# Head pairs on alternating halves of the array, split step sums and later gates in a two-block transformer kernel

## The reference, cut to what matters

```python
proj = u @ w_in
z, xbc, dt_raw, v = split(proj)              # gates, convolution input, steps, pooled input
xbc = silu(causal_depthwise_conv(xbc, conv_w, conv_b))
xs, bm, cm = split(xbc)                      # 16 heads of 64; B and C: 2 groups of 128
dt = softplus(dt_raw + dt_bias); a = -exp(a_log)
a_cs = cumsum(dt * a) in each chunk of 128   # 4 chunks
seg = exp(where(causal, a_cs[l] - a_cs[s], -inf))
y_diag = (C B^T * seg) @ (xs * dt)
y_off  = (C * exp(a_cs)) @ state carried from the chunks before
y = (y_diag + y_off + d_skip * xs) * silu(z)
y_ssd = rmsnorm(y, ssd_norm)
y_pool = multi_scale_pool(v, pool_w, pool_scale)
return concatenate([y_ssd, y_pool]) @ w_out
```

## Time and profile before

| what | value |
|---|---|
| median of 3 runs | 2312.72 us (2311.17 to 2314.09) |
| profiled execution, its own time | 2313.4 us |
| its span | 2311.5 us |
| mean granted PE clock | 0.988 of full speed |
| busy: PE, DVE, ACT, POOL | 97%, 54%, 37%, 14% |

### The profile page before, as it was taken

One profiled execution on the slowest core, in us unless ns is written; L12 is line 12 of the kernel. 1 busy time (PEld: TensorE's weight loads), 2 busy tenths in 40 slices (PEclk: granted clock), 3 DMA queues, 4 the chain that ended last, 5 costly groups with the idle time before them and its releaser, 6 DMA issues. The chain is left out here.

```text
span 2311.5 us, 28724 instructions
## 1 busy us (share of the span) xinstructions
PE 2239.9 (97%) x11284; PEld 1778.9 (77%) x11284; DVE 1248.6 (54%) x1966; ACT 844.3 (37%) x1410; POOL 322.5 (14%) x320
## 2 busy tenths in 40 slices
PE   8899999989999999999999999999999999999998
PEld 6778778858888887877678888887775568888887
DVE  5766566354544445266635454554547874555454
ACT  4433554234222224355532222233135654222223
POOL 1300351001000003032210000010035541000001
PEclk9999999999999999999999999999989999999999
DMA  5232114403333332311123333333230003333231
GB/s 161 73 109 82 47 56 134 121 27 92 94 98 94 98 96 77 91 55 43 31 73 100 101 92 100 93 99 97 91 92 2 2 10 92 99 93 101 91 100 46
DMA packets 292661, 188.08 MB, mean 81 GB/s; under 512 B 7856, under 2 KB 286640, under 8 KB 292528
## 3 DMA queue, kind: packets, MB, share of 16 engines
q1 hardware_dynamic: 292240, 186.05, 26.9%
q10 hardware_dynamic: 288, 0.21, 0.0%
HBM read 184.14 MB, written 2.10 MB: 81 GB/s over the span
## 5 line engine op out<-in xcount | busy, mean ns | idle before, releaser
L470 DVE TENSOR_TENSOR wl<-raw,wh 128x1024 fp32r<-128x1024 f32 x336 | 414.4, 1234 | 715.2 <-ACT wh L460 715.1
L460 ACT CAST wh<-raw 128x1024 fp32r<-128x1024 f32 x336 | 349.6, 1041 | 689.7 <-PE ps L474 674.1
L474 PE MATMUL ps<-xb_x,wh 128*128 128x512 f32 (+1 forms) x1488 | 462.0, 392 | 0.0
L474 PE MATMUL ps<-XH,wh 128*128 128x512 f32 x872 | 348.3, 399 | 10.7 <-issue 4.0
L474 PE MATMUL ps<-XH,wl 128*128 128x512 f32 x872 | 342.1, 392 | 0.0
L474 PE MATMUL ps<-XL,wh 128*128 128x512 f32 x872 | 341.9, 392 | 0.0
L474 PEld LDWEIGHTS ps<-xb_x,wh 128*128 128x128 f32 (+1 forms) x1488 | 277.9, 187 | 59.6
L474 PE MATMUL ps<-xb_x,wl 128*128 128x512 f32 (+1 forms) x744 | 291.7, 392 | 0.0
L564 POOL TENSOR_TENSOR acc<-acc,sq 128x512 f32<-128x512 f32 x55 | 76.1, 1383 | 1338.9 <-ACT sq L551 1337.6
L474 PEld LDWEIGHTS ps<-XH,wh 128*128 128x128 f32 x872 | 165.2, 189 | 47.7 <-issue 8.7
L474 PEld LDWEIGHTS ps<-XH,wl 128*128 128x128 f32 x872 | 165.2, 189 | 35.6
(11 more groups left out here) (341 smaller groups left out, 3455.3 us busy)
## 6 DMA issues: line engine op xcount, KB each, us to landing
raw<-in_mlp_w SPq DMA_DIRECT2D x128, 512.0 KB, 3.7
raw<-in_w_gate_up SPq DMA_DIRECT2D x44, 512.0 KB, 3.7
raw<-in_w_in SPq DMA_DIRECT2D x29, 512.0 KB, 3.6
raw<-in_sb_w_qkv SPq DMA_DIRECT2D x24, 512.0 KB, 3.7
raw<-in_w_down SPq DMA_DIRECT2D x22, 512.0 KB, 3.3
raw<-in_w_out_mix SPq DMA_DIRECT2D x16, 512.0 KB, 4.0
raw<-in_w_kv SPq DMA_DIRECT2D x16, 512.0 KB, 3.8
raw<-in_nsa_w_kv SPq DMA_DIRECT2D x12, 512.0 KB, 3.5
```

The costliest lines, as they stand in the source:

```text
L460: e.copy(shaped(WH[i % NH], i), shaped(RAW[i % NR], i)).then_inc(*w_hi.up(i))
L470: e.tensor_tensor(shaped(WL[i % NH], i), shaped(RAW[i % NR], i), shaped(WH[i % NH], i).bitcast(F), ALU.subtract).then_inc(*w_lo.up(i))
L474: return e.matmul(out, a, b, start=start, stop=stop, skip_group_check=True)
```

## The change

- The units and jobs xbc8 to xbc11 come ahead of the first pool products (they came behind them).
- `NM` is one lower: the main loop ends with z1. z2 goes ahead of the states, z3 and z4 between them; z5, z6 and z7 (`ZF`) are projected in the head loop, half of one (12 matmuls) in each even step from 0 to 10, into the bank `NB`, between `pe_head_a` and `pe_head_m`. Their scaled values go straight into `zt` (steps 3, 7 and 11), and one Silu over 128x3x512 is made in step 12.
- `pe_head_a` makes the sums from a high and a low part of the steps, `ah` and `al`, against an fp32r copy `tur` of the triangle: eight matmuls in place of four in fp32. Three small DVE instructions at dt make the parts.
- `pe_head_b` runs once per pair, in odd steps from 3 to 17, and alternates the two heads for each matmul. The products `eb` and `sg` are freed by pair.
- DVE's `dve_head_y` moves to even steps from 4 (the last behind the loop); POOL's squares move from even steps to odd ones from 5; ACT's and DVE's splitting of y (`act_y`, `dve_y`) moves from steps 4, 6, ... to steps 11 to 17, one pair in each.
- The bank of the sum of squares is planned behind the head loop.

```diff
@@ -340,9 +340,9 @@
-    unit_pool(0)
     for k in range(8, 12):
         unit(f"xbc{k}", wcols(w_in_, 1024 + 128 * k))
+    unit_pool(0)
     unit_out_pool(0)
@@ -717,23 +717,26 @@
     dtt = ph.sb("dtt", [128, 10, 64])
+    adt = Pair(ph.sb("ah", [128, 4, 16], R), ph.sb("al", [128, 4, 16], R))
+    tur = ph.sb("tur", [128, 128], R)
     early = Phase(PH0 + 4 * 8 * S * 4, "mv")
...
     JM = [("dt",)] + [("v", k) for k in range(8)]
+    JM += [("xbc", k) for k in range(8, 12)]
     JM += [("pool", g, m) for g in (0, 1) for m in range(2)]
-    JM += [("xbc", k) for k in range(8, 12)]
     JM += [("op", 0, o, m) for o in range(4) for m in range(2)]
...
     JM += [("z", k) for k in range(8)]
-    NM = len(JM) - 5
+    NM = len(JM) - 6
+    ZF = [5, 6, 7]
     LAG = 4
-    NZ = {k: NM - 3 + k for k in range(8)}
+    NZ = {k: NM - 2 + k for k in range(8)}
     NOP = {half: max(n for n, j in enumerate(JM) if j[:2] == ("op", half)) for half in range(2)}
@@ -752,7 +755,7 @@
             plan(tmp.next(), ("co", n), (a_made, ("conv", a[0])))
-        elif kind == "z":
+        elif kind == "z" and a[0] not in ZF:
             plan(sqr.next(), ("zt", n), (a_made, ("z", a[0])))
@@ -775,6 +778,10 @@
     NCG = [(c, g) for c in range(3) for g in range(2)]
+    def z_of(h):
+        return (ZF[h // 4] if h < 12 and h % 2 == 0 else None), h % 4 // 2
@@ -810,22 +817,21 @@
         tmp8 = Ring(tmp.bufs + scr)
-        plan_sum("y")
         for h in range(18):
-            if h < 2:
-                plan(five.next(), ("mix", NM + 3 + h), mix_bank_freed(NM + 3 + h))
-            if h in (1, 2):
-                plan_mix_evict(NM + 2 + h)
+            z, half = z_of(h)
+            if z is not None and half == 0:
+                plan(NB, ("mix", NZ[z]), mix_bank_freed(NZ[z]))
             if h < 16:
                 plan(five.next(), ("hs", h), (a_made, ("seg", h)))
-                plan(tmp8.next(), ("eb", h), (mixed, ("y", h)))
+                plan(tmp8.next(), ("eb", h), (mixed, ("y", h // 2)))
             if 1 <= h < 17:
-                plan(tmp8.next(), ("sg", h - 1), (mixed, ("y", h - 1)))
-            if h >= 2 and h % 2 == 0:
+                plan(tmp8.next(), ("sg", h - 1), (mixed, ("y", (h - 1) // 2)))
+            if h >= 3 and h % 2:
                 plan(PS[5 + (h // 2 - 1) % 2], ("yb", h // 2 - 1), (v_made, ("yd", h // 2 - 1)))
-            if h >= 4 and h % 2 == 0:
+            if h >= 5 and h % 2:
                 plan_square("y", h // 2 - 2)
         plan_square("y", 7)
+        plan_sum("y")
         tmp.i = 0
@@ -872,11 +878,12 @@
     def pe_head_a(e, h):
-        adt = tv(1)
         t = take(e, ("hs", h))
-        e.wait_ge(*v_made.at("dt"))
+        e.wait_ge(*v_made.at("adt"))
         for c in range(4):
-            f = mm(e, t[:, 128 * c:128 * c + 128], adt[:, c, h:h + 1].to_broadcast([128, 128]), con("TU"), c == 0, False)
+            out = t[:, 128 * c:128 * c + 128]
+            mm(e, out, adt.hi[:, c, h:h + 1].to_broadcast([128, 128]), tur[:, :], c == 0, False)
+            f = mm(e, out, adt.lo[:, c, h:h + 1].to_broadcast([128, 128]), tur[:, :], False, False)
         f.then_inc(*scored.up("a", h))
@@ -886,20 +893,42 @@
-    def pe_head_b(e, h):
-        g, p0 = h // 8, 64 * (h % 2)
-        o = take(e, ("yb", h // 2)) if h % 2 == 0 else got(("yb", h // 2))
-        eb, sg = got(("eb", h)), got(("sg", h))
-        e.wait_ge(*g_made.at("ce", h))
-        e.wait_ge(*v_made.at("segcb", h))
-        e.wait_ge(*v_made.at("xc", h // 2))
+    def pe_head_b(e, j):
+        g, o = j // 4, take(e, ("yb", j))
+        heads = (2 * j, 2 * j + 1)
+        for h in heads:
+            e.wait_ge(*g_made.at("ce", h))
+            e.wait_ge(*v_made.at("segcb", h))
+        e.wait_ge(*v_made.at("xc", j))
         e.wait_ge(*v_made.at("prev", 2, g))
         for c in range(4):
-            out = o[p0:p0 + 64, 128 * c:128 * c + 128]
-            f = mm(e, out, xc[:, c, 64 * h:64 * h + 64], sg[:, 128 * c:128 * c + 128], c == 0, c == 0)
+            at = slice(128 * c, 128 * c + 128)
+            for m, h in enumerate(heads):
+                f = mm(e, o[64 * m:64 * m + 64, at], xc[:, c, 64 * h:64 * h + 64], got(("sg", h))[:, at], c == 0, c == 0)
             if c:
-                f = mm(e, out, prev[:, c - 1, 64 * h:64 * h + 64], eb[:, 128 * c:128 * c + 128], False, True)
-        f.then_inc(*mixed.up("y", h))
+                for m, h in enumerate(heads):
+                    f = mm(e, o[64 * m:64 * m + 64, at], prev[:, c - 1, 64 * h:64 * h + 64], got(("eb", h))[:, at],
+                           False, True)
+        f.then_inc(*mixed.up("y", j))
+    def pe_mix_z(e, h):
+        z, half = z_of(h)
+        if z is None:
+            return
+        n, i = NZ[z], UI[f"z{z}"]
+        t = take(e, ("mix", n)) if half == 0 else got(("mix", n))
+        e.wait_ge(*w_lo.at(i))
+        wh, wl = shaped(WH[i % NH], i), shaped(WL[i % NH], i)
+        for k in range(4 * half, 4 * half + 4):
+            mm(e, t[:, :], wh[:, k, :], X.hi[:, k, :], k == 0, False)
+            mm(e, t[:, :], wh[:, k, :], X.lo[:, k, :], False, False)
+            f = mm(e, t[:, :], wl[:, k, :], X.hi[:, k, :], False, k == 7)
+        if half:
+            f.then_inc(*proj.up("mix", n))
+            if not proj.final:
+                proj.name("unit", i)
@@ -928,14 +957,13 @@
         for h in range(18):
-            if h < 2:
-                pe_mix_job(e, NM + 3 + h)
             if h < 16:
                 pe_head_a(e, h)
+            pe_mix_z(e, h)
             if 1 <= h < 17:
                 pe_head_m(e, h - 1)
-            if h >= 2:
-                pe_head_b(e, h - 2)
+            if h >= 3 and h % 2:
+                pe_head_b(e, h // 2 - 1)
         pe_.end("heads")
@@ -1009,10 +1037,12 @@
         for h in range(18):
-            if h < 2:
-                act_weights(e, UI[mix_unit(NM + 3 + h)] + 2)
-            if h in (1, 2):
-                act_mix_evict(e, NM + 2 + h)
+            z, half = z_of(h)
+            if z is not None and half == 0:
+                act_weights(e, UI[f"z{z}"] + 2)
+            if h == 12:
+                e.wait_ge(*v_made.at("scaled", NZ[7]))
+                e.activation(zt[:, 5:8, :], zt[:, 5:8, :], ACT.Silu).then_inc(*a_made.up("z", 7))
             if h < 16:
@@ -1026,8 +1056,8 @@
                 f.then_inc(*a_made.up("seg", b))
-            if h >= 4 and h % 2 == 0:
-                act_y(e, h // 2 - 2)
+            if h >= 11:
+                act_y(e, h - 11)
         act_y(e, 7)
@@ -1072,8 +1102,8 @@
         else:
-            t = take(e, ("zt", n))
-            scaled(e, "n1", t[:, :], bank).then_inc(*v_made.up("scaled", n))
+            t = zt[:, a[0], :] if a[0] in ZF else take(e, ("zt", n))[:, :]
+            scaled(e, "n1", t, bank).then_inc(*v_made.up("scaled", n))
@@ -1106,6 +1136,11 @@
             e.scalar_tensor_tensor(tv(1), tv(0), -1.0, av, ALU.mult, ALU.mult).then_inc(*v_made.up("dt"))
+            e.wait_ge(*v_made.at("dt"))
+            e.tensor_copy(tur[:, :], con("TU"))
+            e.tensor_copy(adt.hi[:, :, :], tv(1)).then_inc(*v_made.up())
+            e.wait_ge(*v_made.now())
+            e.tensor_tensor(adt.lo[:, :, :], tv(1), adt.hi[:, :, :].bitcast(F), ALU.subtract).then_inc(*v_made.up("adt"))
         elif kind == "v":
@@ -1163,12 +1198,12 @@
     def dve_head_y(e, j):
-        e.wait_ge(*mixed.at("y", 2 * j + 1))
+        e.wait_ge(*mixed.at("y", j))
         e.wait_ge(*a_made.at("conv", j))
...
         e.wait_ge(*v_made.at("yd", j))
-        e.wait_ge(*a_made.at("z", j))
+        e.wait_ge(*a_made.at("z", 7 if j in ZF else j))
         e.tensor_tensor(xsf[:, j, :], xsf[:, j, :], zt[:, j, :], ALU.mult).then_inc(*v_made.up("y", j))
@@ -1212,16 +1247,18 @@
         for h in range(18):
-            if h < 2:
-                dve_weights(e, UI[mix_unit(NM + 3 + h)] + 2)
-            if h in (1, 2):
-                dve_mix_evict(e, NM + 2 + h)
+            z, half = z_of(h)
+            if z is not None and half == 0:
+                dve_weights(e, UI[f"z{z}"] + 2)
+            if h in (3, 7, 11):
+                dve_mix_evict(e, NZ[ZF[h // 4]])
             if 1 <= h < 17:
                 dve_head_m(e, h - 1)
-            if h >= 2 and h % 2:
-                dve_head_y(e, h // 2 - 1)
             if h >= 4 and h % 2 == 0:
-                dve_y(e, h // 2 - 2)
+                dve_head_y(e, h // 2 - 2)
+            if h >= 11:
+                dve_y(e, h - 11)
+        dve_head_y(e, 7)
         dve_y(e, 7)
@@ -1318,7 +1355,7 @@
                 act_root(e, "y")
-                act_rs(e, "y", [(v_made, ("scaled", NM + 4))])
+                act_rs(e, "y", [(v_made, ("scaled", NZ[7]))])
             if o >= 1:
```

## The result

The changed kernel takes **2323.03 us** (median of 4 runs, 2322.22 to 2324.15), the kernel before in the same session 2312.91; the ratio is 1.0042, with an interval of 1.0029 to 1.0056. So it is slower, by some 10 us, where 2317.2 (2302 to 2324) was forecast. The profiled execution took 2322.22 us with a span of 2320.4, against 2313.4 and 2311.5 before. "Cold" stands for matmuls at the lower of the two granted clocks (1.2 GHz; records of 0.63 us for 128x512), "warm" for those at the upper one (2.4 GHz; 0.39 us).

The account below looks back on a forecast made before the run. PE, busy 97% of the span, was taken to bound the kernel. Front +8.3, dt's parts +0.7 and heads -4.5 gave +4.5 us, forecast 2317.2 us from the 2312.7 median; range 2302 to 2324, own range 2311 to 2321.

Parts of the forecast that it names:

- The front: Up to op0's end: four convolution steps ahead of the pool evictions delay op0 from 133.8 to 142.1, +8.3 us.
- dt's parts: Three small DVE instructions at dt in the front join the same saturated chain: +0.7 us (0 to 1).
- Rival 1: Front: the DVE and ACT loop is not the limit and xbc jobs fill PE's gap, front -4, 2304 us; chance 0.20.
- The start of the heads: First head starts at 248.0 - 5.9 + 2.9 = 245.0 us, before the front's shift.
- +2.9 us of new waits: Ahead of the first head, PE waits about 1.4 us for the last Silu and 1.5 for POOL's first decay product.
- The sums: Head step sums in pe_head_a: eight fp32r matmuls limited by weight loads take 0.9 us, nothing gained.
- The values by pairs: In pe_head_b, a pair's 28 records take 1.85 us against 3.34, 12 us less PE work over eight pairs.
- Rival 3: Head values: alternating halves does not overlap, up to 12 us return to PE, 2323 us; chance 0.04.
- The stall: Ahead of each pair's values, PE waits 1.4 us for ACT's exponentials and DVE's product behind the mask.
- Rival 2: Heads: DVE's product behind the mask runs near 1.7 us, not 1.1, in all eight pairs; 2321.7 us; chance 0.22.
- POOL is the limit as it is now: From head 12's exponential, POOL's products set the tail: 13.0 us, then the last values of 1.85.
- cost nothing on PE: Splits of y gathered behind head 11 lie beside the last values and first output projection; about 1.5 us if uncovered.

Follow-up runs that it names:

- experiment 1: Kernel before with only the order of xbc8 to xbc11 swapped ahead of the pool projections; 2321.23 us, ratio 1.0031.
- experiment 6: Also f0_defer: kernel after with the old xbc8 to xbc11 order and dt's three DVE operations moved into the main loop; 2313.52 us, ratio 0.9999.
- experiment 3: Kernel after with the dt sums in the eighth bank, a bank of their own; 2317.53 us, ratio 1.0013.
- experiment 4: As e2_no_swap, with the seven splits of y on ACT and DVE moved behind the last mask work; 2316.01 us, ratio 1.0008.
- f3_gate_first: As f1_lag, with the first half gate put ahead of the first head's sums; 2309.03 us, ratio 0.9989.
- f5_warm: As f3_gate_first, plus 32 matmuls that nobody reads where PE stands in the late heads; 2309.27 us, ratio 0.9984.
- experiment 8: Also x1_no_squares: as experiment 6, with POOL's squares and additions for tiles 3 to 6 cut to 16 of 512 columns; 2311.43 us, ratio 0.9998.
- e2_no_swap: Kernel after with the old order of xbc8 to xbc11, all else of the change kept; 2314.77 us, ratio 1.0006.
- f1_lag: As experiment 6, with each pair's values issued one head step later, ahead of the half gate; 2311.36 us, ratio 0.9989.
- experiment 11: As f3_gate_first, with xbc8 alone also put ahead of the pool projections; 2309.12 us, ratio 0.9991.

## Why the prediction was right or wrong

**The front was right.** Forecast +8.3 for the swap and +0.7 for dt's parts, measured +9.15 together. The third pool job waits to 112.70 (111.9 + 0.7), cold behind, the first op0 job ends at 123.75 (122.8 + 0.7), the last at 142.97 (142.1 + 0.7). Alone the swap is +8.33 (experiment 1). On top of it dt's parts add 0.82; in the old order they are 0.3 us and, in the two traces that have them, 1.3 us of cold records that one trace without them shows too (experiment 6). What was named as cause holds in part: the bank of the dt sums makes 3.6 us of the delay (experiment 3), and for the rest the loop ahead of the evictions is argued from the waits. Rival 1 (the front gains) is out.

**The start of the heads** was forecast at 245.0 + 9.0 = 254.0; it is 255.46, 1.3 us late once the front's 0.15 is taken off. "+2.9 us of new waits" had 1.4 for ACT and 1.5 for POOL, and the trace has 1.24 (229.53) and 0.45 + 0.79 (the second at 237.97); not in the list was the 1.97 us for DVE behind the last state product (0.65 before).

**The sums** cost as forecast: 8 matmuls in 0.94 us (0.9).

**The values by pairs** cost as forecast: 28 records in 1.68 us (1.55 + 0.3). Rival 3 is out. The Trainium skill (TensorE: Matmul & The Clock Gate, Part 3: Packing small matmuls) lets a weight load pass a running matmul only where the row group differs; this trace disagrees again, at 0.055 to 0.06 us per record with only the columns differing.

**The stall** was 1.4 us per pair by forecast and 0.91 to 1.25 (mean 1.05) in the first five; the 1.7 us that this saves went to the cold first half gate, which was not foreseen. So the exponential of head 12 starts 50.2 us after the first sums and ends at 50.8 (50.3 forecast). This is close by luck: two misses of 1.6 to 1.7 us cancel, and the wide Silu took 1.49 us (1.65 forecast). Rival 2 had the right engine and the wrong place: the product is not near 1.7 in all pairs.

**The step that failed** is "POOL is the limit as it is now", with its 13.0 us. From the end of that exponential to the last values it took 16.0 us (306.22 to 322.25), 2.4 more than 0.6 + 13.0, and the values then took 3.2 cold, not 1.85: head stage 70.0 us in place of 65.8. POOL stood 2.01 us for y ahead of 309.57. In its place the trace has two things. From the seventh pair's values to the last's (315.11 to 322.25) it is 7.1 us, and DVE runs back to back: two products, two passes of y and two splits, four of the six slowed beside POOL. From the sixth pair's values to the seventh's (308.25 to 315.11) it is 6.9 us, and there DVE has a gap: the chain runs through PE's values, cold at 3.09 us, its sums, ACT's exponentials and DVE's product.

Neither sum was made. The prediction had counted the seven gathered splits as "cost nothing on PE", hidden by os0; they stand instead between the products, and moved behind the heads they cost the same there (experiment 4). But DVE is not the only limit, for with it relieved the stretch hardly shortens. From the first mask product behind the Silu to the last values it is 16.0 us in the kernel after, f0_defer, f3_gate_first and f5_warm, 15.8 without the squares, with PE cold (experiment 8), and 15.25 without the splits, with POOL last (experiment 4). DVE's passes, the chain through a cold PE and POOL lie within 0.8 us of each other; how far the stretch would fall with all three relieved stays open.

**Behind the heads** os0 runs cold as well: the sum of squares comes 6.88 us after os0's start, 5.57 before, +1.3. At 358.56 the kernel after is 11.4 us late, at its end 8.9; where the 2.5 us come back stays open.

**In all**: forecast +4.5, measured +10.1 by the medians, 8.8 by the two profiled executions. At os0 forecast and trace part by 1.3 (start) + 4.2 (stage) + 0.15 = 5.6 us. The direction came from the front, which was right; the heads, forecast at -4.5 us, gave nothing. The own range of 2311 to 2321 was missed, and 2323.0 lies in the wide one, 2302 to 2324, only near its end.

## What to carry to other kernels

Work taken from the busiest engine is worth only the part that its neighbours can follow: write down the busy sum of each engine per step of the new loop, with the durations that hold beside the others' work, and the chain of hand-offs beside it, before a saving is booked. When steps are gathered for want of a buffer, put them into the sum of the stage in which they land. A job that must evict through a serial loop on other engines should not stand behind more of that loop's work.

## What the runs showed of the hardware

The same wait does not always cost the clock. Behind the same idle time of 1.97 us the first half gate ran with records of 0.44 us (2.8 us in all) in e2_no_swap and x1_no_squares, and began with records of 0.56 to 0.72 (4.4 us) in the kernel after, f0_defer and f1_lag. Behind the same wait of 1.65 us for DVE in op0 (117.4 to 117.8) the first record took 0.50 us in the kernel before, 0.64 in f0_defer and 0.80 in f3_gate_first, though the last two have the same front, and op0 ended 1.4 us later in the last. And behind a wait of 3.18 us the same work took 88.35 us in one kernel and 89.88 in another (experiment 11). So a difference of one or two microseconds between two traces can be the clock alone, and one trace of each kernel is too few to price a change of that size.

A pass of DVE over 128x512 with its operands in SBUF takes 0.68 to 0.74 us where POOL does nothing, and 1.5 to 1.76 in the rows of the tail where a pass of POOL was under way when it started (310.07 and 311.52). What starts first matters: the split at 309.41, 0.16 us ahead of POOL's square, took 0.74, and the square 1.48 where it takes 1.04 by itself. DVE's sum with the skip term, which reads PSUM, takes 0.73 to 0.75 either way (308.03 without POOL, 314.88 and 325.55 beside it).
